# The relative line written from all partitions, and the ring's tiles asked for by GpSimd's own queue

## The chip, the cores and the metric

The kernel runs on one core of a Trainium2 chip. The core has five engines with an instruction queue each: TensorE (PE), VectorE (DVE), ScalarE (ACT), GpSimd (POOL) and SyncE (SP), and sixteen DMA engines, which serve what SP, ACT and POOL ask for. The metric is the device time of one launch in microseconds. The profile and the trace come from one profiled execution of the kernel before.

## The reference

Two blocks in fp32, one after the other, on 256 tokens of width 2048. The first is a modulated transformer block with two kinds of attention and a gated FFN, the second a layer with three branches, one of them cross attention to a memory of 256 tokens. What bears on the change:

```python
mod = silu(c) @ w_ada[l] + b_ada[l]            # c: one row of 2048; w_ada: 2048 x 12288
sh1, sc1, gt1, sh2, sc2, gt2 = split(mod, 6)
h = rms_norm(x, g_norm1[l]) * (1 + sc1) + sh1
proj = h @ w_in[l]                             # 2048 x 3904
logits = einsum(q, k) * scale + rel_bias[t5_bucket(k_pos - q_pos)]   # 8 heads, 256 x 256
x = x + gt1 * (mix @ w_out[l])
...
k = rms_norm(mem_2, mem_norm_g) @ xa_wk        # 2048 x 1024, second block
v = rms_norm(mem_2, mem_norm_g) @ xa_wv
```

The bias of a head depends only on the distance of key and query. So it is one line of 511 values (of 512) per head, and a row of the 256 x 256 bias is a stretch of that line, shifted by one per query.

## The kernel before

**Weights.** All weights stream from HBM once, in tiles of 512 KB. A tile that TensorE multiplies (kind "g", 128 partitions x 2 x 512) lands in one of four slots of `raw`. ScalarE rounds it into `w_hi` (L1049), VectorE takes the rest, raw - w_hi, into `w_lo` (L1596), and TensorE does 12 matmuls on it (L516), one unit: for two token tiles and two k-steps each of w_hi x_hi, w_hi x_lo, w_lo x_hi. `w_hi` and `w_lo` have four slots too, so VectorE and ScalarE run at most four units ahead.

**The modulation.** `w_ada` has one row of inputs only, so VectorE does it: a tile of `w_ada` (128 x 1024) times c_act[k], added to `acc` or `acc_b` (L1616, the first of 16 by L1620). This is a fold. Twelve sums of 16 folds make the 12288 columns, and `sum_ada` on TensorE adds each over the partitions. Sums 0 to 6 and 8, 9 take their tiles through `ring`, which has four slots of its own (kind "b"); sums 7, 10, 11 take them through raw slots (kind "a").

**Order.** Strings say in which order kinds follow, and all engines walk the same strings: `"b" * 16`, then `B2 = "bbg" * 8` for three blocks of xa_wk and xa_wv (24 groups "bbg"), eight "g" for the fourth, then `w_in` in eight blocks, the first by PARTS6 (six "gb", two "g"), the others by B6 (8 g, 6 b). Later `w_out` has D_LATE and D_EVEN. `load` on SyncE issues all these tiles in that order from one queue: a ring tile waits for `ring_used`, a raw tile for `raw_used` (both counted up by VectorE), and what stands behind a waiting issue waits too (L376 the ring, L389 raw).

**Start.** ScalarE squares m_tok (mem_2), GpSimd makes the inverse root (`inverse_root`, L2546 and L2547), VectorE scales m_tok (`scale_tokens`, L1670), TensorE turns it, and ScalarE (`high`) and VectorE (`low`, L1643) split it into x_hi and x_lo, with a fold of VectorE between two low parts. The same is done for x_tok, whose inverse root is GpSimd's second.

**The line.** TensorE makes it from rel_bias and a one-hot table in `psum[0:HD]`, eight partitions, HD = 8 (L586), VectorE copies it to `rb_line` (8 x 512, L1682). GpSimd, behind both roots and the load of gate_row, writes it to DRAM 128 times over (L2555):

```python
pool.dma_start(line_dram, rb_line[:, :].unsqueeze(1).to_broadcast([HD, P, W])).then_inc(line_out, 16)
```

Two reads with a row step of W - 1 bring it back as `bias_t` (L2561) once `chunks_taken` shows that the last low part of x_tok is done. Attention uses it from 428 us on.

**w_out.** After the last head GpSimd loads x for the residual (L2579), which VectorE awaits before its first tile of w_out. SyncE waits for the same moment (head_done), since ring and head data share memory, and then sends ring tiles again for sums 8 and 9.

## Time and profile before

| | us |
|---|---|
| median of 3 runs (lowest, highest) | 2394.75 (2394.46, 2396.35) |
| profiled execution | 2394.84 |
| its span | 2393.1 |
| busy: PE, DVE, ACT, POOL | 2159.8, 1555.4, 990.1, 155.8 |

DMA moved 490.18 MB, 205 GB/s over the span. The mean TensorE clock granted was 0.958 of full speed.

The span is what the trace covers; the profiled execution is 1.7 us longer. A busy engine need not be the one that ends last: that is read from the chain of waits and from what ended the idle time ahead of an instruction. The three stretches that the change touches are 0 to 220 us (mem_2 through xa_wk and xa_wv), 228 to 401 us (w_in) and 611 to 718 us (w_out).

### The profile page before, as it was taken

How to read it: one execution, taken by the hardware profiler on the slowest of the kernel's cores; microseconds unless marked ns; L12 is line 12 of the kernel's file. 1: busy time of each engine (PE TensorE's matmuls, PEld its weight loads, DVE VectorE, ACT ScalarE, POOL GpSimd, SP SyncE). 2: the span in 40 equal slices, each digit the busy share in tenths (PEclk: the TensorE clock that was granted, in tenths of full speed). 3: DMA queues.
4: the chain of work that ended last, by engine and by line, in shares of the span. 5: the costliest groups of instructions: out<-in, count | busy, mean ns of one | idle time of the engine just before them, and what ended most of it. 6: DMA issues, size and time to landing. Idle time of an engine off the chain costs nothing.

```text
span 2393.1 us, 26655 instructions
## 1 busy us (share of the span) xinstructions
PE 2159.8 (90%) x9742; PEld 1746.6 (73%) x9742; DVE 1555.4 (65%) x1688; ACT 990.1 (41%) x1266; POOL 155.8 (7%) x212
## 2 busy tenths in 40 slices
PE   3468997476798999999999999999999999999997
PEld 2356786454577888888888888878687777888886
DVE  6486876655587775545555555568868788865554
ACT  3124444453335334433444445543343434444443
POOL 2000001101000000000000000720202000000000
PEclk9689998687899999999999999999999999999999
DMA  9787995140786886555765556655444555556553
GB/s 323 215 306 252 367 347 199 63 158 1 270 318 234 274 280 208 190 185 186 211 193 184 192 185 206 207 172 180 159 143 156 169 184 167 188 180 239 185 185 132
DMA packets 223774, 490.18 MB, mean 205 GB/s; under 512 B 15834, under 2 KB 18240, under 8 KB 222384
## 3 DMA queue, kind: packets, MB, share of 16 engines
q1 hardware_dynamic: 218080, 467.20, 57.7%
q0 software_dynamic: 4624, 17.16, 2.6%
q10 hardware_dynamic: 960, 4.35, 0.5%
q8 instruction: 69, 1.13, 0.2%
q14 instruction: 41, 0.34, 0.0%
HBM read 482.35 MB, written 6.29 MB: 204 GB/s over the span
## 4 chain that ended last, share of the span: by engine, by line
PE 75%; DVE 10%; DMA 7%; ACT 3%; issue 3%; POOL 1%; DVEq 0%; SPq 0%; ACTq 0%; POOLq 0%
PE psum L516 69%; DVE w_lo L1596 3%; DVE acc L1616 2%; ACT w_hi L1049 2%; DMA ring<-in_w_ada 1%; DMA raw<-in_w_gate 1%; PE psum L639 1%; DVE acc_b L1616 1%; DMA raw<-in_xa_wk 1%; DMA raw<-in_xa_wv 1%; DMA raw<-in_w_out 1%; PE psum L787 1%; PE psum L473 1%; PE psum L827 1%; DMA raw<-in_w_in 1%
## 5 line engine op out<-in xcount | busy, mean ns | idle before, releaser
L1596 DVE TENSOR_TENSOR w_lo<-raw,w_hi 128x1024 fp32r<-128x1024 f32 (+1 forms) x698 | 853.7, 1229 | 661.1 <-ACT w_hi L1049 638.9
L1049 ACT ACTIVATE w_hi<-raw 128x1024 fp32r<-128x1024 f32 (+1 forms) x698 | 735.9, 1056 | 1173.5 <-PE psum L516 891.9
L516 PE MATMUL psum<-w_hi,x_hi 128*128 128x512 f32 (+1 forms) x2048 | 816.6, 399 | 86.7 <-DVE w_lo L1596 86.6
L516 PE MATMUL psum<-w_hi,x_lo 128*128 128x512 f32 (+1 forms) x2048 | 801.7, 391 | 0.0
L516 PE MATMUL psum<-w_lo,x_hi 128*128 128x512 f32 (+1 forms) x2048 | 801.5, 391 | 0.0
L516 PEld LDWEIGHTS psum<-w_hi,x_hi 128*128 128x128 f32 x2048 | 389.2, 190 | 182.5 <-DVE w_lo L1596 74.0
L516 PEld LDWEIGHTS psum<-w_lo,x_hi 128*128 128x128 f32 x2048 | 388.6, 190 | 82.1
L516 PEld LDWEIGHTS psum<-w_hi,x_lo 128*128 128x128 f32 x2048 | 389.6, 190 | 78.4 <-issue 1.0
L516 PE MATMUL psum<-w_hi,f_hi 128*128 128x512 f32 x352 | 140.2, 398 | 0.0
L516 PE MATMUL psum<-w_lo,f_hi 128*128 128x512 f32 x352 | 139.5, 396 | 0.0
L516 PE MATMUL psum<-w_hi,f_lo 128*128 128x512 f32 x352 | 139.5, 396 | 0.0
L1616 DVE SCALAR_TENSOR_TENSOR acc<-ring,c_act,acc 128x1024 f32<-128x1024 f32 x75 | 96.0, 1280 | 17.4 <-DMA ring<-in_w_ada 14.7
L1616 DVE SCALAR_TENSOR_TENSOR acc_b<-ring,c_act,acc_b 128x1024 f32<-128x1024 f32 x60 | 76.8, 1279 | 2.8 <-DMA ring<-in_w_ada 1.3
L516 PEld LDWEIGHTS psum<-w_lo,f_hi 128*128 128x128 f32 x352 | 66.3, 188 | 16.1
L516 PEld LDWEIGHTS psum<-w_hi,f_lo 128*128 128x128 f32 x352 | 66.3, 188 | 15.8
L516 PEld LDWEIGHTS psum<-w_hi,f_hi 128*128 128x128 f32 x352 | 66.3, 188 | 15.8
L516 PE MATMUL psum<-w_hi,yo_hi 128*128 128x512 f32 x192 | 76.5, 398 | 0.0
L516 PE MATMUL psum<-w_lo,yo_hi 128*128 128x512 f32 x192 | 76.1, 396 | 0.0
L516 PE MATMUL psum<-w_hi,yo_lo 128*128 128x512 f32 x192 | 76.0, 396 | 0.0
L1616 DVE SCALAR_TENSOR_TENSOR acc<-raw,c_act,acc 128x1024 f32<-128x1024 f32 x45 | 57.8, 1285 | 7.7 <-DMA raw<-in_w_ada 2.8
L516 PE MATMUL psum<-w_hi,m_hi 128*128 128x512 f32 x128 | 50.9, 398 | 0.0
L516 PE MATMUL psum<-w_lo,m_hi 128*128 128x512 f32 x128 | 50.7, 396 | 0.0
(361 smaller groups left out, 1734.8 us busy)
## 6 DMA issues: line engine op xcount, KB each, us to landing
raw<-in_w_in SPq DMA_DIRECT2D x264, 512.0 KB, 3.9
ring<-in_w_ada SPq DMA_DIRECT2D x144, 512.0 KB, 6.3
raw<-in_w_gate SPq DMA_DIRECT2D x88, 512.0 KB, 3.7
raw<-in_w_up SPq DMA_DIRECT2D x88, 512.0 KB, 4.4
raw<-in_w_down SPq DMA_DIRECT2D x88, 512.0 KB, 3.5
raw<-in_w_out SPq DMA_DIRECT2D x64, 512.0 KB, 4.2
raw<-in_w_ada SPq DMA_DIRECT2D x48, 512.0 KB, 4.5
raw<-in_w_branch SPq DMA_DIRECT2D x48, 512.0 KB, 4.3
```

The lines of the kernel that those rows point to most:

```text
L473: last = pe.transpose(psum[0:src.shape[1], bank, j * P:j * P + r], src, ident[0:r, 0:r])
L516: last = pe.matmul(pair(b)[:, a, 0:width], x[:, k, cut], w[:, s, kk, 0:width], start=(u == 0 and kk == 0 and n == 0), stop=(u == units - 1 ...
L639: last = pe.matmul(psum[:, bank, i * width:(i + 1) * width], wT[:, kt * SEQ + i * P:kt * SEQ + (i + 1) * P], value(kt), start=(kt == 0), s ...
L787: last = pe.transpose(to[:, j * P:(j + 1) * P], src, ident[:, :])
L827: last = pe.matmul(psum[:, 6 + j, ri * SEQ:(ri + 1) * SEQ], bT[rows, ri, f, :], uT[rows, f, :], start=True, stop=True)
L1049: act.activation(w_hi[:, s, :, 0:width], raw[:, r, :, 0:width], ACT.Copy).then_inc(hi_ready, 1)
L1596: dve.tensor_tensor(w_lo[:, s, :, 0:width], raw[:, r, :, 0:width], w_hi[:, s, :, 0:width].bitcast(F32), ALU.subtract).then_inc(raw_used, 1)
L1616: last = dve.scalar_tensor_tensor(to, src, c, to, ALU.mult, ALU.add)
```

## The change

1. Ring tiles are issued by GpSimd (`load_ring`), in pieces set between its other work: 4 first of all, 4 after a new copy, 12 between the two roots, 44 after the line, 48 after the bias reads, 32 after the load of x for w_out. SyncE's queue has raw tiles only.
2. The line is made on 128 partitions: GpSimd copies rb_rows into `rb_wide` with each head 16 times, TensorE's product then fills 128 partitions, and each partition writes its line 8 times, where each of 8 wrote it 128 times. VectorE's copy has 128 partitions instead of 8, and stands after folds 5 to 8 instead of before them.
3. ScalarE scales m_tok and x_tok instead of VectorE.
4. The six folds in the first block of w_in move into blocks 1 to 6 (B7 has 7 b), and two sums are taken up at other blocks.

```diff
+B7 = "gbgbgbgbgbgbgbg"
-PARTS6 = ["gb"] * 6 + ["g"] * 2
...
-            rb_line = sb("rb_line", [HD, W], stack=ph)
+            rb_line = sb("rb_line", [P, W], stack=ph)
...
+            load("g" * 96, ahead)
+            pl.step("fold", KD * BY_RING)
             load(A8)
...
-            pe.matmul(psum[0:HD, 7, :], rb_rows[:, :], onehot[:, :], start=True, stop=True).then_inc(line_summed, 1)
+            pe.wait_ge(heads_spread, 1)
+            pe.matmul(psum[:, 7, :], rb_wide[:, :], onehot[:, :], start=True, stop=True).then_inc(line_summed, 1)
...
-            turn_and_multiply(x_tok, PARTS6)
+            turn_and_multiply(x_tok, "g")
...
-                multiply(B6)
-                if b in (2, 5, 7):
+                multiply(B7 if b < 7 else B6)
+                if b in (3, 5, 7):
...
+            act.wait_ge(norm_given, 1)
+            for a in range(TT):
+                act.activation(m_tok[:, a, :], m_tok[:, a, :], ACT.Copy, scale=stats[:, 0, a:a + 1]).then_inc(mem_scaled, 1)
...
-            split(G8)
+            split(S0)
+            act.wait_ge(norm_given, 2)
+            for a in range(TT):
+                act.activation(x_tok[:, a, :], x_tok[:, a, :], ACT.Copy, scale=stats[:, 1, a:a + 1]).then_inc(x_scaled, 1)
+            split(S0)
...
+            def load_ring(n):
+
+                for _ in range(n):
+                    k, c, s = pl.n["fold"] % KD, pl.n["fold"] // KD * AW, pl.slot("ring", RING)
+                    pool.wait_ge(ring_used, pl.at("ring", 1))
+                    pool.dma_start(ring[:, s, :], w_ada[:, k, c:c + AW]).then_inc(ring_landed[s], 16)
+                    pl.step("ring")
+                    pl.step("fold")
+
+            load_ring(RING)
...
+            pool.wait_ge(small_in, 16 * SMALL_DMAS)
+            pool.tensor_copy(rb_wide[:, :].rearrange("p (h j) -> p h j", h=HD),
+                             rb_rows[:, :].unsqueeze(2).to_broadcast([32, HD, P // HD])).then_inc(heads_spread, 1)
+            load_ring(4)
             inverse_root(0, TT, D)
+            load_ring(KD - 4)
             inverse_root(1, TT, D)
...
-            pool.dma_start(line_dram, rb_line[:, :].unsqueeze(1).to_broadcast([HD, P, W])).then_inc(line_out, 16)
+            pool.dma_start(line_dram.rearrange("h (j r) n -> (h j) r n", r=HD),
+                           rb_line[:, :].unsqueeze(1).to_broadcast([P, HD, W])).then_inc(line_out, 16)
+            load_ring(4 * KD - RING - KD)
```

GpSimd's queue from its first root to the bias reads, before. `stats` are the sums of squares, the TENSOR_TENSOR is the power that makes the root; rel_line is the line in DRAM.

```order
L2546 TENSOR_SCALAR stats<-stats 128x2 [waits norm_asked,consts_set]
L2547 TENSOR_TENSOR stats<-stats,neg_half 128x2 [waits pool_link]
L2546 TENSOR_SCALAR stats<-stats 128x2 [waits norm_asked]
L2547 TENSOR_TENSOR stats<-stats,neg_half 128x2 [waits pool_link]
L2553 DMA gate_row<-in_b_ada 128x2048
L2555 DMA rel_line<-rb_line 1024x1x512 [waits line_set]
L2561 DMA bias_t<-rel_line 128x8x256 [waits chunks_taken,line_out]
```

And the same place after:

```order
L2572 COPY rb_wide<-rb_rows 32x128 [waits small_in,consts_set]
L2537 DMA ring<-in_w_ada 128x1024 [waits ring_used] x4
L2566 ISA
L2566 TENSOR_SCALAR stats<-stats 128x2 [waits norm_asked]
L2567 TENSOR_TENSOR stats<-stats,neg_half 128x2 [waits pool_link]
L2537 DMA ring<-in_w_ada 128x1024 [waits ring_used] x12
L2566 TENSOR_SCALAR stats<-stats 128x2 [waits norm_asked]
L2567 TENSOR_TENSOR stats<-stats,neg_half 128x2 [waits pool_link]
L2578 DMA gate_row<-in_b_ada 128x2048
L2580 DMA rel_line<-rb_line 1024x1x512 [waits line_set]
L2537 DMA ring<-in_w_ada 128x1024 [waits ring_used] x44
L2588 DMA bias_t<-rel_line 128x8x256 [waits chunks_taken,line_out]
```

Ring tiles 5 to 8 now stand behind the arrival of the small loads and ahead of the first root, tiles 9 to 20 between the roots, and tile 21 behind gate_row and the line. The next piece, 48 tiles, stands behind the bias reads.

VectorE near the start, before: from its small columns to the first low part of m_tok.

```order
L1680 TENSOR_SCALAR comb<-cols 128x1 [waits chunks_taken]
L1682 COPY rb_line<-psum 8x512 [waits line_summed,dve_link]
L1685 TENSOR_TENSOR lv_rows<-lv_rows 128x2x64
L1686 TENSOR_REDUCE lam<-lv_rows 128x2 [waits dve_link]
L1616 SCALAR_TENSOR_TENSOR acc_b<-ring,c_act,acc_b 128x1024 [waits ring_used,ring_landed0]
```

After:

```order
L1691 TENSOR_SCALAR comb<-cols 128x1 [waits chunks_taken]
L1633 SCALAR_TENSOR_TENSOR acc_b<-ring,c_act,acc_b 128x1024 [waits ring_used,ring_landed0,dve_link]
L1633 SCALAR_TENSOR_TENSOR acc_b<-ring,c_act,acc_b 128x1024 [waits ring_used,ring_landed1]
L1633 SCALAR_TENSOR_TENSOR acc_b<-ring,c_act,acc_b 128x1024 [waits ring_used,ring_landed2]
L1633 SCALAR_TENSOR_TENSOR acc_b<-ring,c_act,acc_b 128x1024 [waits ring_used,ring_landed3]
L1694 COPY rb_line<-psum 128x512 [waits line_summed]
L1697 TENSOR_TENSOR lv_rows<-lv_rows 128x2x64
L1698 TENSOR_REDUCE lam<-lv_rows 128x2 [waits dve_link]
```

The copy of the line and the lambda rows (`lam`, which ScalarE awaits before it begins on m_tok's high parts) stand behind the folds of tiles 5 to 8 now.

## Rows read from the trace of the kernel before

**Rows 1.** The page: the chain that ended last, shares by engine.

```profile
PE 75%; DVE 10%; DMA 7%; ACT 3%; issue 3%; POOL 1%; DVEq 0%; SPq 0%; ACTq 0%; POOLq 0%
```

**Rows 2.** Stretches of 20 us: busy us (instructions), clock, DMA share, GB/s.

```profile
60.00:80.00 20.00, 4.58 (x12) 3.34 (x12) 7.16 (x9) 1.06 (x1) 0.00 (x0) 0.64 0.76 162
80.00:100.00 20.00, 4.93 (x12) 3.57 (x12) 3.34 (x3) 1.06 (x1) 0.00 (x0) 0.59 0.64 138
...
300.00:320.00 20.00, 20.00 (x90) 16.56 (x89) 15.41 (x14) 7.43 (x7) 0.00 (x0) 1.00 1.02 375
```

**Rows 3.** The chain of waits in time: start, length, what it was.

```profile
63.61 35.53 DMA ring<-in_w_ada
```

**Rows 4.** Short stretches: PE, PEld, DVE, ACT, POOL busy, clock, DMA share, GB/s.

```profile
92.00:96.00 4.00, 3.75 (x9) 2.97 (x10) 0.36 (x2) 0.00 (x0) 0.00 (x0) 0.50 0.51 79
...
262.00:264.00 2.00, 0.81 (x4) 0.39 (x3) 1.48 (x2) 0.48 (x1) 0.00 (x0) 1.00 1.04 396
...
2388.00:2390.00 2.00, 0.00 (x0) 0.00 (x0) 1.76 (x2) 0.00 (x0) 0.00 (x0) 0.50 1.02 406
```

**Rows 5.** GpSimd's timeline: start, length, line, what, idle before and its releaser.

```profile
22.57 0.71 POOL L2547 TENSOR_TENSOR stats<-stats,neg_half 128x2 f32<-128x2 f32 x1
...
51.26 1.13 POOL L2555 DMA_DIRECT2D rel_line<-rb_line  x1
246.02 1.83 POOL L2561 DMA_DIRECT2D bias_t<-rel_line  x2 [193.63 <-DVE x_lo L1643]
...
1402.30 0.68 POOL L2593 DMA_DIRECT2D x_kept<-x  x1 [250.23 <-DVEq L1967]
```

**Rows 6.** DMA issues: count, KB each, median us from issue to landing.

```profile
ring<-in_w_ada SPq DMA_DIRECT2D x144, 512.0 KB, 6.3
...
rel_line<-rb_line POOLq DMA_DIRECT2D x1, 2048.0 KB, 47.6
bias_t<-rel_line POOLq DMA_DIRECT2D x2, 1024.0 KB, 11.4
...
x_kept<-x POOLq DMA_DIRECT2D x4, 512.0 KB, 3.1
```

**Rows 7.** VectorE's timeline, with columns as in rows 5.

```profile
21.55 0.68 DVE L1682 COPY rb_line<-psum 8x512 f32<-8x512 f32 x1 [7.42 <-PE psum L586]
...
28.02 2.47 DVE L1670 TENSOR_SCALAR m_tok<-m_tok,stats 128x2048 f32<-128x2048 f32 x2
...
45.89 0.68 DVE L1643 TENSOR_TENSOR x_lo<-turned,x_hi 128x512 fp32r<-128x512 f32 x1
...
99.17 1.28 DVE L1616 SCALAR_TENSOR_TENSOR acc<-ring,c_act,acc 128x1024 f32<-128x1024 f32 x1 [2.05 <-DMA ring<-in_w_ada]
101.54 1.23 DVE L1596 TENSOR_TENSOR w_lo<-raw,w_hi 128x1024 fp32r<-128x1024 f32 x1 [1.08 <-ACT w_hi L1049]
...
134.00 2.67 DVE L1616 SCALAR_TENSOR_TENSOR acc_b<-ring,c_act,acc_b 128x1024 f32<-128x1024 f32 x2
...
191.75 5.15 DVE L1596 TENSOR_TENSOR w_lo<-raw,w_hi 128x1024 fp32r<-128x1024 f32 x4
...
620.80 4.63 DVE L1596 TENSOR_TENSOR w_lo<-raw,w_hi 128x1024 fp32r<-128x1024 f32 x4 [9.80 <-DMA x<-in_x]
```

**Rows 8.** TensorE's timeline: the line's product, and two turnings of x_tok.

```profile
19.58 1.87 PE L586 MATMUL psum<-onehot,rb_rows 32*8 32x512 f32 x2 [6.08 <-DMA rope<-in_sin]
...
237.04 0.60 PE L562 MATMUL psum<-ident,x_tok 128*128 128x128 f32 x4
...
240.22 0.60 PE L562 MATMUL psum<-ident,x_tok 128*128 128x128 f32 x4
```

**Rows 9.** ScalarE's timeline: the first high part, the last square of x_tok.

```profile
31.77 0.84 ACT L1065 ACTIVATE turned<-psum,cols 128x256 f32<-128x256 f32 x2 [8.79 <-PE psum L473]
...
47.62 1.91 ACT L1113 ACTIVATE junk<-x_tok 128x2048 f32<-128x2048 f32 x1
```

**Rows 10.** What SyncE's queue waited for, 0 to 400 us: total, times, longest.

```profile
SPq L376 <- DVE acc_b L1616: 69.7, 39, 11.4
```

More of the change, by code:

```diff
@@ L367, in _, with walk @@
                 "w_in_2", "glu_w", "w_branch", "w_out_2")}
+            def walk(name, k, c, width=W):
+                while True:
+                    yield name, k, c, width
+                    k += 2
             def load(seg, src=None):
@@ L387, in load, with first_weights @@
                     else:
-                        name, k, c, width = src
+                        name, k, c, width = next(src)
                         sp.dma_start(raw[:, s, :, 0:width], views[name][:, k:k + 2, bass.ds(c, width)]).then_inc(landed[s], 16)
-                        src[1] += 2
                     pl.step("raw")
-            load("b" * KD)
-            for name, c in (("xa_wk", 0), ("xa_wv", 0), ("xa_wk", W)):
-                load(B2, [name, 0, c, W])
-            load(G8, ["xa_wv", 0, W, W])
-            for b in range(8):
-                load(B6, ["w_in", 0, b * W, W if b < 7 else IN1 - 7 * W])
+            def first_weights():
+                for name, c in (("xa_wk", 0), ("xa_wv", 0), ("xa_wk", W), ("xa_wv", W)):
+                    for k in range(0, KD, 2):
+                        yield name, k, c, W
+                for b in range(8):
+                    for k in range(0, KD, 2):
+                        yield "w_in", k, b * W, W if b < 7 else IN1 - 7 * W
+            ahead = first_weights()
+            load("g" * 96, ahead)
+            pl.step("fold", KD * BY_RING)
             load(A8)
             for b in range(3):
-                load("gaga" if b < 2 else "gg", ["w_q_b", 0, b * W, W])
+                load("gaga" if b < 2 else "gg", walk("w_q_b", 0, b * W, W))
             for b in range(4):
-                load("ga", ["w_kv_b", 0, b * W, W])
+                load("ga", walk("w_kv_b", 0, b * W, W))
             for b in range(4):
                 if b == 0:
-                    src = ["w_out", 0, 0, W]
+                    src = walk("w_out", 0, 0, W)
                     load(S0, src)
@@ L445, in _ @@
+                load(S0 + S0, walk("w_out_2", 0, i * 2 * W + W, W))
             for a in range(TT):
@@ L1664, in plain @@
                 pl.step("chunk")
-            def scale_tokens(dst, src, slot, done):
-                dve.wait_ge(norm_given, pl.at("norm", 1))
-                pl.step("norm")
-                for a in range(TT):
-                    dve.tensor_scalar(dst[:, a, :], src[:, a, :], stats[:, slot, a:a + 1], None, ALU.mult).then_inc(done, 1)
             plain([(col("c", 0, KD), 0, KD)])
@@ L1689, in row @@
                 return sm[:, k, :]
-            work("bbbb")
-            scale_tokens(m_tok, m_tok, 0, mem_scaled)
             for k in range(0, KD, 2):
@@ L1697, in _ @@
             take_ada(0)
-            scale_tokens(x_tok, x_tok, 1, x_scaled)
+            pl.step("norm", 2)
             dve.wait_ge(dt_ready, 1)
@@ L1757, in _ @@
                 plain([(mem_kT[:, k:k + 2, :].rearrange("p k t -> p (k t)"), 0, W)])
-            work_now = iter(PARTS6)
-            for k in range(0, KD, 2):
-                low(x_hi[:, k:k + 2, :], x_lo[:, k:k + 2, :], True)
-                work(next(work_now))
+            low_and_work("g", True)
             dve.wait_ge(gate_b_in, 16)
@@ L2564, in _ @@
                 pool.dma_start(pe_gain[:, k, :], t[name][P:P + 64].partition_broadcast(P)).then_inc(pe_in, 16)
+            load_ring(3 * KD)
             inverse_root(3, TT, 512)
@@ L2579, in _ @@
             pool.dma_start(x1[:, :, :], tok_view(t["x"])).then_inc(x1_in, 16)
+            pl.step("fold", KD)
+            load_ring(2 * KD)
             inverse_root(8, TT, D)
```

60 lines of the change are left out of this document (30 added, 30 removed).

## The prediction

> **What bounds the kernel now.** I read the chain of waits first. TensorE has 75% of it, VectorE 10% and transfers 7% [rows 1]. So most of the span runs at TensorE's rate, and an edit pays only where TensorE is not what ends last. The change touches three stretches: 0 to 220 us (projections of mem_2), 228 to 401 us (w_in) and 611 to 718 us (w_out). The stretches in windows say which of them have slack: TensorE is busy 4.6 and 4.9 of 20 us at 60 to 100, and all 20 at 300 to 320 [rows 2]. From 228 to 401 TensorE sets the pace, and before 193 it does not.
>
> The hole at 60 to 100 has one owner. The chain shows a piece of 35.53 us at 63.61 that is the landing of a ring tile [rows 3]. It is not full bandwidth that holds it: the DMA share is 0.66 to 0.76 there and only 138 to 162 GB/s move, and at 92 to 96 us the share is 0.51 with 79 GB/s [rows 2, 4]. Under way all that time is the write of the relative line, asked for by GpSimd at 51.26 [rows 5]: 2 MB, 47.6 us from issue to landing, where a ring tile takes 6.3 [rows 6]. It reads 8 partitions. A share of about half is what eight busy engines of sixteen would give, and every ring and raw tile has a part on those eight.
>
> Outside the hole VectorE sets the pace up to 193 us. One group of two ring tiles and one multiplied tile ("bbg") is 2.67 + 1.23 us, 3.9 in all, where nothing is missing [rows 7]. There are 24. The fifth ends at 102.8 (101.54 + 1.23) and the last at 193.0 (191.75, the first of four, + 1.23) [rows 7]; what follows (8 tiles of 2.73 us on TensorE, then turning) hangs on it with a fixed length.
>
> **The change, part by part.** My times below are on the profiled execution's clock (2393.1 us span, 2394.84 us in all, so 1.7 us lie around it; the median, 2394.75, is the same number for my purpose).
>
> *Start, 0 to 51 us.* GpSimd now issues four ring tiles ahead of its small loads. One issue of 512 KB takes its queue 0.68 us [rows 5], so four are 2.7 us, and the small loads, which TensorE's one-hot product awaited until 19.58 [rows 8], are in at 22.3. The new copy of rb_rows (32x128) has no row; between nothing and the 1.0 us of a root's two instructions I take 0.3. Then tiles 5 to 8 are issued, until 25.3. Formerly these were long in the ring. The root for m_tok, which ended at 23.28 (22.57 + 0.71 [rows 5]) about 1.0 us after it could begin, ends at 26.4, and two scalings on ScalarE, at the 1.91 of a square over the same 128x2048 [rows 9], end at 30.2; VectorE's ended at 28.02 + 2.47 = 30.5 [rows 7]. That edit costs nothing. The folds of tiles 5 to 8 do: first tile asked for at 23.2, landing about 5 us later beside the 2 MB of x_tok, four folds of 1.3 us from 28.2 to 33.4, then the copy of the line (0.68 [rows 7]) and two small instructions on the lambda rows, 1.1 us together. ScalarE waits for these rows before its first high part: 34.8 instead of 31.77 [rows 9], 3.0 late. Eight rounds of fold and low part are VectorE's own 1.28 + 0.68 [rows 7] = 1.96 us instead of the 1.8 that ScalarE and TensorE allow now, 1.3 more over eight. So the squares of x_tok, whose last ended near 49.6 (47.62 + 1.91 [rows 9]), end at 54.0.
>
> *The line, 51 to 68 us.* GpSimd's queue is in order: root of x_tok, gate_row, line, then ring tile 21. Shifted by 4.4 us, gate_row is asked for at 55.0, the line at 55.7, tile 21 at 57.5. Tiles 17 to 20 were asked for before the root, so VectorE works from 51 to 63.0: 0.74 + 1.28, wait for the first high part (54.0 + 1.06), 1.23, 2.67, 1.23, and some 2.8 of state rows; the 2.5 us scaling of x_tok is gone from it. Tile 21 lands behind gate_row (1.05 MB), the line (2.10 MB) and two raw tiles: 4.7 MB with itself. The line is now read from 128 partitions. Its price from both sides: nothing but bandwidth, as the output's writes move 406 GB/s [rows 4], 5.2 us; or the rate that the old write had on its engines, 79 GB/s over eight, twice that on sixteen, 13.3 us. I take the first, as 512 KB writes of 128x512 land in 3.1 us [rows 6]. 4.7 MB at 0.40 MB/us and a little for issue puts tile 21 at 68.3: VectorE idles 5.3 us instead of 29.
>
> *Groups 3 to 24, 68 to 170 us.* Groups 3 to 5 are 11.7 us. For groups 6 to 24 I take the time that they have now, 193.0 - 102.8 = 90.2 us: 19 x 3.9 = 74.1, 12.9 of state rows, sums and a wait for TensorE's turning, all of which stay, and 3.2 of gaps ahead of w_lo, where a raw tile was late behind ring waits. Those 3.2 go. Against them stands the transfers' limit: a group is 1.57 MB, so 3.9 us asks 403 GB/s, more than the 375 of a long full stretch [rows 2] and just the 406 of a short one [rows 4]; I take 3.2 us for it, between 0 and the 6.6 (22 x 0.3) that 375 GB/s would cost. 68.3 + 11.7 + 90.2 = 170.2 against 193.0: **22.8 us gained**. SyncE's ring issues waited 69.7 us for acc_b alone [rows 10], but VectorE's own load covers all of it except those 3.2.
>
> The Trainium skill, page DMA: Bandwidth & Descriptors, section Rules for kernel authors, holds that an outermost dimension of c < 16 confines a DMA to at most c engines; the share of 0.51 agrees, and by it the new write has sixteen engines. The same section says that spreading DMAs over SP, ACT and GpSimd doesn't help bandwidth and saves only issue time; by it the 3.2 us of gaps would stay and the 22.8 be 19.6. The trace half agrees: raw tiles came late because their issue stood behind ring waits, not because the engines were slow.
>
> *w_in.* The first block gives up its six folds. They were covered: TensorE's units with turning repeat every 3.19 us (237.04, 240.22 [rows 8]), VectorE needs 0.68 + 1.23 + 1.28 = 3.19, and TensorE is the one that never idles. Blocks 1 to 6 carry 7 folds instead of 6: 8 x 1.23 + 7 x 1.28 = 18.8 us of VectorE in 21.9 us of TensorE, 7.86 MB or 359 GB/s. Hidden. The new wait is at the border: GpSimd sends no ring tile until the last low part of block 0, because its wait for the bias reads stands ahead of load_ring(48). With u0 the start of the first unit (the last turning at 240.22 [rows 8] less four units and three turnings: 227.9), that low part comes at u0 + 16; the two bias reads (1.83 [rows 5]) and two gains take 2.9 us to issue, and the ring tile lands behind 2 MB that took 11.4 us [rows 6]. With VectorE stopped the raw queue goes quiet after two tiles, so I put tile 65 at u0 + 27.5; one fold and one w_lo give TensorE its unit at u0 + 30.1, and it runs dry at u0 + 4 x 3.19 + 5 x 2.73 = 26.4. Stall 3.6 us, bounds 0 (bias at full rate) and 8 (behind 11.4 us and pe_gain); now it is 1.2 (0.81 busy of 2.00 at 262 to 264 [rows 4]). **2.4 us lost.**
>
> *w_out.* VectorE waits 9.8 us for x, until 620.8, while two ring tiles share the engines [rows 7]. Now x is first in GpSimd's queue and the ring behind it: 1 MB less ahead, 2 us gained, bounds 0 and 2.5. Raw tiles no longer follow ring waits: VectorE's gaps ahead of w_lo are 0.2 to 1.3 us here, of which I take 1.5, bounds -1 and 4. **3.5 us gained.** The last GpSimd root there stands behind load_ring(32), whose last issue precedes the last fold by four: no cost.
>
> Sum: -22.8 + 2.4 - 3.5 = -23.9, so 2394.8 - 23.9 = **2370.9 us**.
>
> **The rivals.** *Ring turnaround (13%).* A slot now passes through GpSimd: 0.7 issue + landing + 1.3 fold must fit the 7.8 us of two groups, so landing must be under 5.8 us. The ring's median was 6.3 [rows 6], with six tiles in flight. At 7 us the cycle is 9.0, 1.2 more over 11 pairs: 13 us, giving 2384. Page SBUF — State Buffer of the Trainium skill (the box on the trap "DVE blocks DMA") says that VectorE in a two-port mode keeps GpSimd from writing descriptors; the trace has such candidates only in the folds that start a sum, one in 16, so the rule adds little. Against it: 512 KB lands in 3.1 us when engines are not full.
>
> *The line stays slow (5%), the case on the other side.* If the speed of the old write was set by something other than its 8 partitions, it still takes 47.6 us, and ring tiles are now in the same queue behind it: tile 21 at 55.7 + 48 = 104 rather than 68.3. That is 36 us on the sum: 2406. It decides from a write of 29 us (5.2 + 23.9) on, where the gain is used up.
>
> *The border of w_in (12%).* The stall is 10 to 12, not 3.6: 2378.
>
> *More than said (7%).* Two queues keep the engines full and the 3.2 us of saturation go and the idle at 63 shrinks, w_out gains 4 more: 2360.
>
> *No change (3%).* Turnaround cycle near 9.9 us: the gain is spent in groups 3 to 24.
>
> **How the numbers follow.** Forecast 60%, 2364 to 2377. Rivals 13, 5, 12, 7, 3. The range leaves out the slow line and the flat case: 2358 to 2387. About 0.2% (5 us) is what a measurement can tell here from no change. Faster by more: 60 + 13 + 12 + 7 = 92%; within: 3%; slower: 5%.
>
> **What would show it.** In the changed profile: the line's landing under 15 us; VectorE idle about 5 us before the fold of tile 21 near 68; the last low part of m_tok near 51; the 24th group's end near 170 and the x_tok turning near 200; TensorE idle 2 to 6 us once, some 27 us into w_in; VectorE's first w_lo of w_out 2 us sooner after head_done. Wrong if VectorE's waits ahead of folds repeat every fourth tile (turnaround), or if small_in comes much after 22 us.

## The result, and the profile after the change

The changed kernel takes 2385.88 us (median of 7 runs, 2384.94 to 2387.2) against 2394.75 (median of 7 runs of the kernel before on the same chip, 2391.78 to 2399.88): a ratio of 0.9962, with a 95% interval from 0.995 to 0.9973. It is 8.9 us faster. The forecast was 23.9 us faster. So the sign is right, and 8.9 of the 23.9 us came: the time lies outside the 2364 to 2377 us that had 60%, and inside the full range of 2358 to 2387. The profiled execution took 2386.94 us with a span of 2385.2, against the span of 2393.1 before.

The hole that the change was aimed at is gone. Transfers issued from 50 to 73 us in the changed kernel (count, KB each, median us from issue to landing):

```profile
ring<-in_w_ada POOLq DMA_DIRECT2D x6, 512.0 KB, 14.9
rel_line<-rb_line POOLq DMA_DIRECT2D x1, 2048.0 KB, 13.6
gate_row<-in_b_ada POOLq DMA_DIRECT2D x1, 1024.0 KB, 6.7
```

The line's write took 47.6 us [rows 6] and takes 13.6. VectorE waited through a landing of 35.53 us [rows 3]; in its timeline (start, length, line, what, idle before and who ended it) it now waits 8.39 for tile 21 of the ring, and the last low part of the 24th group is the first of the four that start at 172.51, so it ends at 173.7 instead of 193.0 [rows 7]:

```profile
72.61 2.69 DVE L1633 SCALAR_TENSOR_TENSOR acc<-ring,c_act,acc 128x1024 f32<-128x1024 f32 x2 [8.39 <-DMA ring<-in_w_ada]
...
172.51 4.63 DVE L1613 TENSOR_TENSOR w_lo<-raw,w_hi 128x1024 fp32r<-128x1024 f32 x4
```

So 19.3 us are won by 174 us. At the end 7.9 are left. The rest is lost at places that the same trace shows. The first is the start. TensorE's timeline: the small rows are there at 22.21. GpSimd's: it copies the heads at 23.90, and only then asks for ring tiles 5 to 8.

```profile
22.21 0.39 PE L482 MATMUL psum<-ident,b_rows 96*128 96x96 f32 x1 [17.29 <-DMA v_rows<-in_ssm_d]
```

```profile
23.90 0.28 POOL L2572 COPY rb_wide<-rb_rows 32x128 f32<-32x128 f32 x1 [9.40 <-DMA rope<-in_sin]
24.37 2.12 POOL L2537 DMA_DIRECT2D ring<-in_w_ada  x4 [0.19 <-issue]
...
57.29 0.92 POOL L2580 DMA_DIRECT2D rel_line<-rb_line  x1
```

The folds of those four tiles stand on VectorE ahead of the small instructions for which ScalarE waits. ScalarE's first high part comes at 37.80 instead of 31.77 [rows 9], and everything up to the line is 6.0 us late: the line is issued at 57.29 instead of 51.26 [rows 5].

```profile
37.69 0.20 ACT L1141 ACTIVATE lam<-lam 128x2 f32<-128x2 f32 x1 [6.04 <-DVE lam L1698]
37.80 0.82 ACT L1075 ACTIVATE turned<-psum,cols 128x256 f32<-128x256 f32 x2
```

The second is the border after the first block of w_in. GpSimd waits for the last low part of that block, reads the bias and the gains, and only then asks for ring tile 65. VectorE gets it at 240.83, after 12.30 us of nothing. First GpSimd's timeline, then VectorE's:

```profile
226.27 1.80 POOL L2588 DMA_DIRECT2D bias_t<-rel_line  x2 [62.19 <-DVE x_lo L1660]
228.07 0.56 POOL L2591 DMA_DIRECT2D pe_gain<-in_g_q_mla  x1
228.62 0.55 POOL L2591 DMA_DIRECT2D pe_gain<-in_g_k_mla  x1
229.16 2.11 POOL L2537 DMA_DIRECT2D ring<-in_w_ada  x4
```

```profile
240.83 0.75 DVE L1637 TENSOR_SCALAR acc_b<-ring,c_act 128x1024 f32<-128x1024 f32 x1 [12.30 <-DMA ring<-in_w_ada]
```

TensorE stands for 5.88 us after its last multiplication, as its timeline shows first. The same stretch in windows follows (us; then busy time and instructions of TensorE, its weight loads, VectorE, ScalarE and GpSimd; granted clock; DMA share; GB/s). TensorE starts again at a granted clock of 0.50, which is the lower of its two levels, 1.2 GHz:

```profile
242.77 0.79 PE L525 MATMUL psum<-w_hi,x_hi 128*128 128x512 f32 x1 [5.88 <-DVE w_lo L1613]
```

```profile
238.00:242.00 4.00, 0.00 (x0) 0.00 (x0) 1.17 (x2) 1.48 (x2) 0.12 (x1) 0.65 1.03 412
242.00:246.00 4.00, 3.23 (x8) 2.56 (x9) 4.00 (x4) 0.00 (x0) 0.94 (x2) 0.50 0.98 367
246.00:250.00 4.00, 4.00 (x19) 3.28 (x18) 4.00 (x5) 1.06 (x1) 1.06 (x2) 1.00 1.02 380
```

From the issue of the bias reads to the end of w_in (GpSimd's root at L2566) it takes 392.29 - 226.27 = 166.02 us; before it was 403.64 - 246.02 = 157.62. At the end of w_in the lead over the kernel before is down from 19.7 to 11.3. Three rows of GpSimd's timeline mark the rest: end of w_in, load of x, root of x1.

```profile
392.29 0.19 POOL L2566 TENSOR_SCALAR stats<-stats 128x2 f32<-128x2 f32 x1 [18.03 <-ACT squares L1186]
...
600.46 0.80 POOL L2607 DMA_DIRECT2D x<-in_x  x1 [60.80 <-DVE x_lo L1806]
...
719.07 0.19 POOL L2566 TENSOR_SCALAR stats<-stats 128x2 f32<-128x2 f32 x1 [23.79 <-DVE stats L1995]
```

The third loss seems to be w_out: from the load of x to the root of x1 the changed kernel takes 118.61 us, the one before 115.85, where 3.5 us were to be won. What comes after is the same in both (1666.13 and 1665.95 us).

### The profile page after: what moved, and what is told of

Its sections match the earlier page's. It is cut to its first block, busy times and chain, and to the rows that moved or that the text cites. A ratio compares the mean times of both kernels' runs of the same rounds, so it can differ in the third digit from the quotient of the medians.

```text
span 2385.2 us, 26656 instructions
## 1 busy us (share of the span) xinstructions
PE 2166.2 (91%) x9742; PEld 1753.0 (73%) x9742; DVE 1548.9 (65%) x1684; ACT 997.6 (42%) x1270; POOL 233.9 (10%) x357
## 3 DMA queue, kind: packets, MB, share of 16 engines
q1 hardware_dynamic: 197344, 391.69, 51.7%
## 4 chain that ended last, share of the span: by engine, by line
PE 76%; DVE 10%; DMA 7%; ACT 3%; issue 2%; POOL 1%; DVEq 0%; ACTq 0%; PEldq 0%; POOLq 0%; SPq 0%
PE psum L525 70%; DMA ring<-in_w_ada 4%; DVE w_lo L1613 2%; DVE acc L1633 2%; DMA raw<-in_w_out 1%; ACT w_hi L1059 1%; PE psum L649 1%; DMA raw<-in_w_gate 1%; PE psum L797 1%; DVE acc_b L1633 1%; PE psum L482 1%; PE psum L837 1%; PE psum L721 0%; DMA rope<-in_sin 0%; PE psum L722 0%
## 5 line engine op out<-in xcount | busy, mean ns | idle before, releaser
L2537 POOL DMA_DIRECT2D ring<-in_w_ada x144 | 77.3, 539 | 298.6 <-DVE acc L1633 140.3
L1633 DVE SCALAR_TENSOR_TENSOR acc_b<-ring,c_act,acc_b 128x1024 f32<-128x1024 f32 x60 | 76.8, 1279 | 19.9 <-DMA ring<-in_w_ada 19.3
```

Of the source, the lines that this page charges most:

```text
L1633: last = dve.scalar_tensor_tensor(to, src, c, to, ALU.mult, ALU.add)
L2537: pool.dma_start(ring[:, s, :], w_ada[:, k, c:c + AW]).then_inc(ring_landed[s], 16)
```

## The experiments

The theory after the result: the fast line brings what was forecast or a little more, and giving the ring to GpSimd's queue costs it again, since that queue is worked in order and the ring now stands behind things that have nothing to do with it (and small loads behind the ring). The rivals: the two parts need each other; or the losses lie elsewhere (TensorE's clock, bandwidth), and the queue only stands beside them.

All times are medians; the kernel before was run beside each group, 2395.25, 2395.82 and 2396.55 us in the three groups. The changed kernel was 8.9 us under it in the first comparison and 13.2 us in the last group, and was not run in the two groups between. So where a time of those two groups is set against the 2385.88 us of the changed kernel, the difference is uncertain by some 4 us, and the stages read from the traces are the firmer evidence.

### Each part alone

**The line alone**: the kernel before with

```diff
+            pool.wait_ge(small_in, 16 * SMALL_DMAS)
+            pool.tensor_copy(rb_wide[:, :].rearrange("p (h j) -> p h j", h=HD),
+                             rb_rows[:, :].unsqueeze(2).to_broadcast([32, HD, P // HD])).then_inc(heads_spread, 1)
...
-            pool.dma_start(line_dram, rb_line[:, :].unsqueeze(1).to_broadcast([HD, P, W])).then_inc(line_out, 16)
+            pool.dma_start(line_dram.rearrange("h (j r) n -> (h j) r n", r=HD),
+                           rb_line[:, :].unsqueeze(1).to_broadcast([P, HD, W])).then_inc(line_out, 16)
```

and the product and copy that fill 128 partitions.

> The kernel before with only the line's part of the change: the line's rows are made on 128 partitions and written from all of them, while SyncE goes on asking for the modulation tiles of the ring, in the order of need. Theory (the split into two queues costs time at the start, at the border of w_in and in w_out, and the line alone brings the gain): the line lands in 13 to 16 us instead of 47.6, the last low part of the 24th group ends 5 to 6 us sooner than the 173.7 of the changed kernel because the first high part is back at 31.8, the border of w_in and w_out cost what they cost before, and the run takes 2367 to 2374 us. Rival (the queue split carries a part of the gain: with one queue each ring tile that waits for its slot or lands behind the line's write holds SyncE's weights back, as before): the line lands as fast but the 24th group ends at 175 or later and the run takes 2378 to 2388 us.

2369.57 us, ratio 0.9888 [0.9871, 0.9905]: 25.7 us faster than before, 16 faster than the whole change. Its GpSimd asks for the line at 51.71, and for the bias reads at 218.50; transfers issued from 50 to 73 us and VectorE's folds of tiles 21 and 22:

```profile
rel_line<-rb_line POOLq DMA_DIRECT2D x1, 2048.0 KB, 17.3
```

```profile
61.36 2.66 DVE L1619 SCALAR_TENSOR_TENSOR acc<-ring,c_act,acc 128x1024 f32<-128x1024 f32 x2
```

The line lands later than the 13 to 16 us of the theory. Tile 21 costs no wait here and 8.39 us in the changed kernel, where GpSimd asks for it only behind the line, at 58.07; the first wait for a ring tile after the line is 0.36 us, for tile 24. The 24th group ends at 164.9 (163.65, the first of four, + 1.23), 8.8 us sooner than in the changed kernel, where 5 to 6 were expected. Later VectorE waits for high parts instead of ring tiles, so line to bias reads takes 166.8 us here and 169.0 there. The issue order of SyncE, which looked like a burden, holds nothing back that counts.

**The queue alone**: the changed kernel with those lines put back to the write from 8 partitions (the wait for small_in stays, and so do the scaling on ScalarE and the new order of tiles).

> The changed kernel with only the line's part undone: the line is written from 8 partitions as before, the ring stays with GpSimd's queue. Theory (the split costs 6 us at the start, 8 at the border of w_in and 2 to 4 in w_out, and brings nothing that the fast line does not bring): the line lands in about 47 us again, tile 21 of the ring lands some 33 us later than in the changed kernel, at 103 to 108, and the run takes 2405 to 2422 us. Rival (two queues do help while the line is slow, since SyncE's weights no longer stand behind a ring tile, and GpSimd's queue moves the line's packets and the ring's side by side): the run takes 2386 to 2398 us.

2415.91 us, ratio 1.0081 [1.0066, 1.0095]: 20.1 us slower than the kernel before. Transfers issued from 50 to 73 us, and VectorE's fold of tile 21:

```profile
rel_line<-rb_line POOLq DMA_DIRECT2D x1, 2048.0 KB, 44.8
```

```profile
103.54 2.68 DVE L1630 SCALAR_TENSOR_TENSOR acc<-ring,c_act,acc 128x1024 f32<-128x1024 f32 x2 [39.17 <-DMA ring<-in_w_ada]
```

While that write runs with hardly anything beside it, the transfer engines are half busy (a window, columns as above):

```profile
80.00:85.00 5.00, 0.00 (x0) 0.00 (x0) 0.00 (x0) 0.00 (x0) 0.00 (x0) 0.50 0.50 73
```

So what makes the line fast is how it is written, from 128 partitions instead of 8, and not the queues. (The number of partitions and the shape of the transfer's pattern change together; no run separates them.) The two parts help each other little: -25.7 and +20.1 add up to -5.6, the whole change gives -8.9 and, in the last group, -13.2, so 3 to 8 us. While the line is slow, GpSimd's queue makes it worse, as the tile waits for all of it.

### The border of w_in

```diff
-            load_ring(4 * KD - RING - KD)
+            load_ring(4 * KD - RING - KD + RING)
...
-            load_ring(3 * KD)
+            load_ring(3 * KD - RING)
```

> The changed kernel with four more ring tiles asked for ahead of the reads of the line's result, so that GpSimd's queue has them in flight before it waits for the end of the write and issues its ten small loads. Theory (the 12.3 us wait for ring tile 65 at the border of w_in is queue order alone: the tile was asked for at 229.2, behind the bias and gain loads): the wait falls under 3 us, TensorE's longest wait there from 5.9 to under 2 us, w_in ends 5 to 7 us sooner than 392.3, and the run takes 2378 to 2381 us. Rival (the reads of the bias fill the shared DMA engines, and weights of w_in would be late there as well, or the wait at the write's end moves): the wait goes to another tile and the run stays within 2 us of 2385.9.

2377.79 us, ratio 0.9925 [0.991, 0.9941]: 17.5 us under the kernel before, and 8.1 us less than the changed kernel's 2385.88. VectorE's timeline at the border has no wait for a ring tile any more:

```profile
222.00 2.36 DVE L1613 TENSOR_TENSOR w_lo<-raw,w_hi 128x1024 fp32r<-128x1024 f32 x2 [0.26 <-ACT w_hi L1059]
224.28 0.74 DVE L1637 TENSOR_SCALAR acc_b<-ring,c_act 128x1024 f32<-128x1024 f32 x1
```

TensorE's longest wait there is 0.55 us instead of 5.88. Bias reads to end of w_in: 158.81 us instead of 166.02. The order in the queue is the cause, and the traffic of the bias reads is not: they and the ring tiles are as many as before. The gain at the end of w_in, 11.2 us in these two traces, is above the 5 to 7 expected; 7.2 of it is the border. Of the other 4.0, 1.4 are TensorE's clock: its first unit of w_in ran at the lower level in the changed kernel (4.21 us) and at the higher in this one (2.81).

### The start

**Ring tiles 5 to 8 asked for ahead of the wait for the small loads**:

```diff
+            load_ring(4)
             pool.wait_ge(small_in, 16 * SMALL_DMAS)
             pool.tensor_copy(rb_wide[:, :].rearrange("p (h j) -> p h j", h=HD),
                              rb_rows[:, :].unsqueeze(2).to_broadcast([32, HD, P // HD])).then_inc(heads_spread, 1)
-            load_ring(4)
```

> The changed kernel with the issue of ring tiles 5 to 8 moved ahead of GpSimd's wait for the small loads and its copy of the heads. Theory (the first high part came at 37.8 instead of 31.8 since the ring's second four tiles were asked for only after that wait, at 24.4): ring tiles 5 to 8 are asked for from 9 to 20 us on, as their slots come free, are folded by 28, but the small loads still land at 22 behind them; the first high part comes at 33 to 35 and the run takes 2381 to 2384 us. Rival (the start is set by the small loads themselves, which wait in GpSimd's queue behind 2 MB of ring, and more ring tiles ahead of them only delay them): the column loads land later than 22.2, the first high part stays at 37 to 39 and the run takes 2385 to 2388 us.

2379.98 us, ratio 0.9936 [0.9923, 0.995], a little under the 2381 to 2384 of the theory. The first high part came at 34.48 (theory 33 to 35), the line was issued at 53.95 instead of 57.29. The folds of tiles 5 to 8 ended at 33.2, not 28: tiles 7 and 8 were asked for at 17.31 and 21.29 and folded 10.5 and 10.6 us later, beside the load of x_tok, where the changed kernel's tiles took 6.7. The trace explains 3.3 of the 5.9 us between the medians; this kernel's runs spread from 2378.43 to 2387.08, and its profiled execution was one of the long ones.

**The first sum's 16 ring tiles by SyncE**, ahead of its weights, on semaphores of their own (ring_first):

```diff
+                        if pl.n["fold"] < KD:
+                            s = pl.slot("ring", RING)
+                            sp.wait_ge(ring_used, pl.at("ring", 1))
+                            sp.dma_start(ring[:, s, :], views["w_ada"][:, k, c:c + AW]).then_inc(ring_first[s], 16)
+                            pl.step("ring")
...
-            load_ring(RING)
+            pl.step("ring", KD)
+            pl.step("fold", KD)
```

with GpSimd asking for tiles 17 to 20 before the root of x_tok and for none earlier.

> The changed kernel, but the 16 ring tiles of the first sum are asked for by SyncE, ahead of its weights as in the kernel before; GpSimd asks for the others from tile 17 on, so that its small loads stand first in its queue. Theory (the late start was made of two parts: 3.3 us from asking for tiles 5 to 8 late, and the rest from the small loads that waited behind 2 MB of ring): the small loads land at 12 to 14 us instead of 22.2, the first high part comes at 31.5 to 33 instead of 37.8, and the run takes 2379 to 2382 us. Rival (the second part of the delay comes from GpSimd's copy of the heads and its root, or from the scaling on ScalarE): the small loads land early but the first high part stays at 34 or later, and the run takes 2382 to 2386 us.

2378.66 us, ratio 0.9929 [0.9916, 0.9942]. The theory is right on the small rows (12 to 14 us) and was too careful on the rest. TensorE has the small rows at 12.91, and ScalarE's first high part is at 28.07, 9.7 us before the changed kernel and 3.7 before the kernel before:

```profile
12.91 0.40 PE L489 MATMUL psum<-ident,b_rows 96*128 96x96 f32 x1 [7.79 <-DMA v_rows<-in_ssm_d]
```

```profile
22.90 3.90 ACT L1144 ACTIVATE m_tok<-m_tok,stats 128x2048 f32<-128x2048 f32 x2 [1.42 <-POOL stats L2578]
...
28.07 0.84 ACT L1082 ACTIVATE turned<-psum,cols 128x256 f32<-128x256 f32 x2 [1.08 <-PE psum L489]
```

The scaling of m_tok on ScalarE, which the change brought and the prediction had at nothing, runs as soon as the root is there; on VectorE it stood behind folds, until 28.02 + 2.47 [rows 7]. In the changed kernel the late ring hid this gain. The border is untouched in this kernel: 12.43 us for the first ring tile after the bias reads, at 230.75, and 166.04 us to the end of w_in. At the end of w_in it leads the changed kernel by 10.2 us; the medians differ by 7.2.

### The ring of w_out, and the repairs together

**The 32 ring tiles of w_out by SyncE**, on semaphores of their own:

```diff
+                        if pl.n["fold"] // KD in RING_AGAIN:
+                            s = pl.slot("ring", RING)
+                            sp.wait_ge(ring_used, pl.at("ring", 1))
+                            sp.dma_start(ring[:, s, :], views["w_ada"][:, k, c:c + AW]).then_inc(ring_again[s], 16)
+                            pl.step("ring")
...
-            load_ring(2 * KD)
```

> The changed kernel, but the 32 ring tiles of the ninth and tenth sums, those folded during w_out, are asked for by SyncE again, in their places between the weights, as in the kernel before. Theory (in w_out GpSimd's queue fetches ring tiles before they are needed, and they take the shared DMA engines from the weight tiles that are needed first): up to the end of w_in and the load of x nothing changes, from the first low part of w_out (608.8) to the root of x1 it takes 106 us again instead of 110.3, and the run takes 2380 to 2383 us. Rival (w_out took longer because TensorE's granted clock was low there, whatever the queue; or the stretch is bound by its bytes): the stretch stays at 109 to 111 us and the run within 1.5 us of 2385.9.

2385.61 us, ratio 0.9956 [0.9941, 0.9972]. From the first low part of w_out to the root of x1 it took 106.6 us (610.68 to 717.25), as the theory says, but the changed kernel's own second trace took 106.3 there. x came 1.1 us later after its issue, and the run is no shorter: the rival's time. It settles nothing alone.

**Two repairs**, border and tiles 5 to 8:

> The changed kernel with two repairs: four ring tiles ahead of the reads of the line, and ring tiles 5 to 8 ahead of the wait for the small loads. Measured one at a time they gave 8.1 us and 5.9 us against the 2385.9 of the changed kernel. Theory (they act in different stretches, but the trace put only 3.3 us to the second): 2372 to 2376 us. Rival (what is won at the start waits at the border, and only the larger of the two counts): 2377 to 2380 us.

2375.98 us, ratio 0.991 [0.9896, 0.9925]: 9.9 us under the changed kernel. The theory's time. The border is repaired in full (158.32 us from bias reads to end of w_in), and the first high part is at 34.29.

**Three repairs**, with the ring of w_out by SyncE as well:

> The changed kernel with three repairs: four ring tiles ahead of the reads of the line, ring tiles 5 to 8 ahead of the wait for the small loads, and the ring of w_out with SyncE. The two-repair kernel of the same group lacks only the last. Theory (the repairs act in different stretches and add up: 8 at the border, 3 to 6 at the start, 1 to 3 in w_out): 2369 to 2375 us, 1 to 3 us under the kernel with two repairs. Rival (what the order of w_out costs is below what can be seen): the two kernels of the group within 0.7 us of each other.

2372.84 us, ratio 0.9903 [0.9889, 0.9918]; 3.1 us under its neighbour, which is the theory's side, but with overlapping intervals (the runs with two repairs reach from 2368.68 to 2379.48).

### All of it with SyncE, and the measures again

**Every ring tile by SyncE**, the rest of the change kept (fast line, scaling on ScalarE, new order of tiles):

```diff
-            load("g" * 96, ahead)
-            pl.step("fold", KD * BY_RING)
+            load("b" * KD + B2 * 3 + G8 + G8 + B7 * 6 + B6, ahead)
...
+                        s = pl.slot("ring", RING)
+                        sp.wait_ge(ring_used, pl.at("ring", 1))
+                        sp.dma_start(ring[:, s, :], views["w_ada"][:, k, c:c + AW]).then_inc(ring_landed[s], 16)
+                        pl.step("ring")
```

and GpSimd's calls of load_ring taken out.

> The changed kernel with every ring tile asked for by SyncE, in its place between the weights; the fast line, the scaling on ScalarE and the new order of the tiles stay. Theory (nothing in the split pays; the scaling on ScalarE with undisturbed small loads gives 3.7 us at the start, as with the first sum by SyncE, where the first high part came at 28.1 instead of 31.8): first high part at 28 to 29, line issued at 47 to 48, bias reads at 214 to 217, w_in ends at 372 to 375, and the run takes 2364 to 2368 us, 2 to 5 us under the kernel with the line alone in the same group. Rival (the split is worth something between the line and the border, since the kernel with the first sum by SyncE took 168.4 us there and the one with the line alone 166.8): bias reads at 218 or later and 2369 us or more.

2366.56 us, ratio 0.9878 [0.9857, 0.9898]: the lowest of all, 2.6 us under the line alone in the same group, whose interval overlaps. The bias reads at 215.34 and the end of w_in at 373.65 are where the theory has them; the first high part, at 29.64, and the line, at 49.15, come about 1 us later than it says. GpSimd's timeline:

```profile
49.15 0.91 POOL L2580 DMA_DIRECT2D rel_line<-rb_line  x1
...
215.34 1.79 POOL L2587 DMA_DIRECT2D bias_t<-rel_line  x2 [165.28 <-DVE x_lo L1663]
...
373.65 0.19 POOL L2568 TENSOR_SCALAR stats<-stats 128x2 f32<-128x2 f32 x1 [154.92 <-ACT squares L1189]
```

**First sum by SyncE and the border repaired**, the two edits shown above in one kernel:

> The changed kernel with the first sum's ring tiles asked for by SyncE and four more ring tiles ahead of the reads of the line: of the split, only the middle of the cross-attention weights and w_in and the tiles of w_out stay with GpSimd. Theory (start and border are separate losses of 7.2 and 8.1 us against the changed kernel): 2369 to 2373 us, w_in ends at 373 to 376. Rival (a loss that is removed at one place comes back at the next): 2375 to 2379 us.

2367.47 us, ratio 0.9884 [0.9864, 0.9904]. Both losses go, and neither comes back later: bias reads at 215.36, end of w_in at 373.68. It is a little under the theory's 2369 to 2373. The 96 ring tiles of the next six sums still come through GpSimd's queue before the end of w_in and the 32 of w_out; that costs nothing that these runs can tell.

**The line alone once more**, and **the changed kernel once more**, in the same group:

> The kernel before with only the line's part of the change, once more, beside the changed kernel and the two new ones on one chip. Theory: 2366 to 2372 us, 14 to 18 us under the changed kernel. Rival (the 16 us between them were a difference of chips or of calls): under 10 us.

> The changed kernel itself once more, as the measure for the three others on the same chip. Theory: 2383 to 2388 us, as before. Rival (it was measured high or low by chance): outside of that.

2369.16 us (0.9893 [0.9872, 0.9915]) and 2383.37 us (0.9957 [0.9939, 0.9974]). The difference between them is 14.2 us on one chip; it was no matter of chips.

Against the second run of the changed kernel the kernel with every ring tile by SyncE is the cleanest measure of the split, since nothing but the queue of the ring tiles differs and both ran in one group: 2383.37 - 2366.56 = 16.8 us.

### The stages side by side

Worked out from the marks named above in each trace (us). "Line to bias" is from the issue of the line to that of the bias reads, "to w_in's end" from there to GpSimd's root behind w_in, "to x" to the load of x, "w_out" from there to the root of x1.

| kernel | first high part | line issued | line to bias | to w_in's end | to x | w_out | after |
|---|---|---|---|---|---|---|---|
| before | 31.8 | 51.3 | 194.8 | 157.6 | 207.7 | 115.9 | 1666.0 |
| changed | 37.8 | 57.3 | 169.0 | 166.0 | 208.2 | 118.6 | 1666.1 |
| changed, again | 37.6 | 57.1 | 167.1 | 166.0 | 210.3 | 114.6 | 1665.3 |
| queue alone | 38.0 | 57.4 | 200.0 | 166.8 | 211.1 | 116.6 | 1666.8 |
| line alone | 32.2 | 51.7 | 166.8 | 158.3 | 210.7 | 115.8 | 1666.2 |
| line alone, again | 32.6 | 52.1 | 165.5 | 158.0 | 208.6 | 114.6 | 1665.9 |
| border | 37.3 | 56.8 | 165.5 | 158.8 | 208.5 | 118.6 | 1666.8 |
| tiles 5 to 8 | 34.5 | 54.0 | 168.1 | 166.8 | 213.2 | 115.4 | 1668.0 |
| w_out by SyncE | 37.7 | 57.2 | 168.5 | 166.7 | 208.8 | 116.1 | 1668.8 |
| two repairs | 34.3 | 53.8 | 170.4 | 158.3 | 210.6 | 116.2 | 1665.5 |
| three repairs | 34.9 | 54.4 | 168.2 | 158.3 | 210.3 | 112.8 | 1665.2 |
| first sum by SyncE | 28.1 | 47.7 | 168.4 | 166.0 | 208.2 | 115.6 | 1666.4 |
| first sum and border | 28.4 | 47.9 | 167.4 | 158.3 | 209.4 | 115.7 | 1665.6 |
| all by SyncE | 29.6 | 49.2 | 166.2 | 158.3 | 208.5 | 116.4 | 1665.8 |

Three columns carry the story. *To w_in's end* has two values and nothing between: 166.0 to 166.8 in the six traces where ring tile 65 stands behind the bias reads, 157.6 to 158.8 in the other eight. TensorE's wait at the border goes with it, 5.85 to 6.06 us in the six and at most 1.3 in the eight. *Line issued* follows who brings the first ring tiles. *Line to bias* is 194.8 and 200.0 with the slow line and 165 to 170 with the fast one, whoever brings the ring. The column *to x* holds a stretch that no kernel changes, and it differs by 5.5 us between traces; so a difference of 2 or 3 us in one stage of two traces is no evidence.

TensorE's clock has a part in the differences of *line to bias*: its first unit of w_in ran at the lower level in seven of the fourteen traces, the changed kernel's two and one of the line alone's two among them, and takes about 1.4 us longer then.

The third loss has to be read with this care. In w_out the six traces whose ring comes from SyncE have a mean of 115.3 (112.8 to 116.4), the eight others 116.4 (114.6 to 118.6), and the changed kernel's own second trace has 114.6. Cut at VectorE's first low part, the stage says more. From the load of x to that low part the eight take 7.9 to 8.3 us and the six 9.5 to 9.9: there the split gains 1.5 us. From the low part to the root of x1 the eight take 106.3 to 110.7 us, 108.2 on average, and the six 103.1 to 106.6, 105.6 on average: there it loses 2.7. Together that is a cost of about 1 us. What makes up the 2.7 no run shows.

## Why the prediction was right in sign and wrong in size

**The hole and its owner**: right. The write of 2 MB from 8 partitions took 47.6 us, and 44.8 in the queue-alone kernel; from 128 it took 13.4 to 17.3 us in the twelve traces that have it, 13.6 in the changed kernel, under the 15 that the prediction asked for. The Trainium skill, page DMA: Bandwidth & Descriptors, section Rules for kernel authors, has an outermost dimension under 16 confine a DMA to as many engines at most. The traces agree: the DMA share was 0.50 while the write from 8 partitions ran nearly alone in the queue-alone kernel, and 44.8 us became 13.6 in the changed kernel, which differs from it only in how the line is made and written.

**The time of groups 3 to 24**: right. From the start of the fold of tile 21 to the end of the 24th group the prediction had 101.9 us; it took 173.7 - 72.6 = 101.1. Ring turnaround, the rival with 13%, did not come: after tile 21 the waits ahead of folds were 0.3 to 1.7 us, 7.7 in all. Its time, 2384 us, is the nearest of all to the measured one; that is chance. But the 3.2 us of gaps that were to go with the split are not the split's: the line-alone kernel, with SyncE's issue order, takes no longer from line to bias reads (166.8 and 165.5 against 169.0 and 167.1). The gaps ahead of low parts did go, but VectorE waited those 7.7 us for ring tiles in their place, and the line-alone kernel waited 7.4 us ahead of low parts and 0.4 for the ring. The same section of the Trainium skill says that spreading DMAs over more issuing engines brings no bandwidth; the four numbers from line to bias reads agree.

**The start and tile 21, first failed step.** "4.4 us late" was 6.0. The chain was the right one. Three sizes in it were too small: the small loads were all in, and GpSimd's copy began, at 23.90, not 22.3; the first of tiles 5 to 8 was folded 6.7 us after its issue, not 5; and the first high part came at 37.8, not 34.8. One was too large: the eight rounds of fold and low part took no longer than before (from the first high part to the line 19.5 us in both), not 1.3 more. Then tile 21 was folded at 72.6, not 68.3, after 8.4 us of idling, not 5.3. Of these 4.3 us, 1.7 are the late start, as gate_row was asked for at 56.7 and not at 55.0. The other 2.6 are the transfers: "4.7 MB at 0.40 MB/us" took the line at the price of bandwidth alone, the lower of the prediction's two bounds, and while it went out, with gate_row and the ring tiles, the engines moved 277 GB/s at a share of 0.95 from 60 to 64 us, and 415 only after that (windows with columns as above):

```profile
60.00:64.00 4.00, 4.00 (x16) 3.20 (x15) 3.76 (x13) 3.21 (x2) 0.53 (x1) 1.00 0.95 277
64.00:68.00 4.00, 1.44 (x7) 0.86 (x5) 0.22 (x1) 0.00 (x0) 0.00 (x0) 1.00 1.04 415
```

Together, with 0.8 us won back in the groups, the 24th group ended at 173.7, not 170.2: 3.5 us of the miss. A step of the same part was wrong in kind: "that edit costs nothing" for the scaling on ScalarE. It gains about 3 us where the small loads are not held up (first high part 28.1 and 29.6, against 31.8, 32.2 and 32.6 with the scaling on VectorE); the copy of the line was moved in the same kernels, so the gain isn't shown to be the scaling's alone.

**The border of w_in, second failed step.** The place and the mechanism stand in the prediction, the size was wrong. 2.4 us lost were said, a stall of TensorE of 3.6 less the 1.2 of before. The stall was 5.9, and the lower clock behind it, which was no term of the sum, cost 1.5 more (its first eight multiplications took 3.4 us, and eight at the higher level take 1.9): 6.2 us lost. The stage from bias reads to the end of w_in shows 8.4 (166.0 against 157.6), and 7.2 of it came back with the border's repair. The last low part was 16 us into w_in, as said. Tile 65 was folded at 240.8, some 32 us into w_in instead of 27.5: bias reads issued 1.25 us after the low part's start, tile 65 asked for at 229.2 and in VectorE's hands 11.7 us later, where 8.6 were said. The rows had 11.4 us for the bias reads [rows 6]; I had argued it down because VectorE would stand still and the weights' queue go quiet, and the engines were not quiet: the DMA share was 1.03 to 1.04 from 230 to 242. The rival named "the border of w_in" (12%, stall of 10 to 12, 2378 us) has the right place and too long a stall: 5.9 lies between the two, inside the term's bounds of 0 to 8.

**w_out, third failed step.** 3.5 us gained were said. In the profiled execution 2.8 were lost, in the second trace of the changed kernel 1.3 gained. The x part is real in all traces, at about 1.5 us instead of 2 (first low part 7.9 to 8.3 us after the issue of x, against 9.5 to 9.9 with SyncE's ring). The 1.5 us to be gained behind it were a loss of 2.7 on average. 3.5 us were claimed on differences that one trace cannot show.

**The sum.** Against the span that the prediction implied (2393.1 - 23.9 = 2369.2) the profiled 2385.2 is 16.0 us too long: 3.5 up to the 24th group, 5.5 more by the end of w_in (the 1.4 of the clock in the first unit of w_in is among them), 0.5 more by the load of x, 6.3 in w_out, and 0.2 behind it. Of the 6.3, 4.0 are absent from the second trace. The repairs give back the first two terms: with the first sum by SyncE and the border repaired, the kernel is at 2367.5.

**What the prediction never asked** is what the split is good for. Its own sum has 27.2 us for the line (22.8 and the 4.4 of the late start), 4.4 and 2.4 lost by the split, and 3.5 and some of the 3.2 won by it. Priced apart, the parts would have shown that the split had to earn 6.8 us out of small gaps. The line alone measured 25.7 and 27.4 us, and the split, with all else the same, cost 16.8.

## What to carry to other kernels

Before a stream of tiles is given to another engine's queue, write down everything else in that queue in order, with the waits: each tile is now behind all of it (here VectorE stood 12.3 us for a tile asked for behind one wait and four loads), and each small load behind the tiles. Here the stream that one slow transfer held up was freed by making that transfer fast, and splitting the queues had nothing left to win. Where a tile must go through a queue with long waits, have the next slots' worth asked for ahead of the wait.

## What the runs showed of the hardware that I had not expected

- The small rows that TensorE awaits, queued behind four ring tiles (2 MB) in GpSimd's queue, were in 9.3 us later (22.2 against 12.9), though the four issues ahead of theirs took 2.35 us in all; with the tiles in SyncE's queue they came at 12.8 to 14.2. The last of the small loads, on which GpSimd's copy waits, were only 3.6 to 4.5 us later (23.9 against 19.4 to 20.3).
- One issue of a 512 KB ring tile by GpSimd takes 0.53 us when nothing is in the way (2.12 for four), under the 0.68 of the row for x_kept [rows 5].
- Ring tiles that were asked for while m_tok and x_tok landed came slowly: in the kernel that asks early, tiles 5, 7 and 8 were asked for at 14.49, 17.31 and 21.29 us and folded 9.9, 10.5 and 10.6 us later; in the changed kernel the first of tiles 5 to 8, asked for at 24.37, was folded after 6.7.
- After 5.88 us without work TensorE came back at a granted clock of 0.50: eight multiplications in the window from 242 to 246 (3.23 us busy), where 19 fit in the 4 us after that.
